# Reordering the pieces of a Fourier convolution stage, loading its first rows a stage ahead, and a third buffer and a new load order in the stage that prepares its spectra

## The reference, cut to what matters

```python
v, x1, x2 = jnp.split(hy, HYENA_ORDER + 1, axis=-1)
filt = hyena_filters(S, ...)                       # (h @ w3) * decay, [L, 2, 2, 1024]
z = v.astype(f32)
for n, gate in enumerate((x1, x2)):
    k = bidir_kernel(filt[:, n, 0], filt[:, n, 1])
    z = gate.astype(f32) * fftconv(z, k, filt_bias[l, n])
```

## Time and profile before

| | |
|---|---|
| three runs | 4445.9, 4446.94, 4450.4 us; median 4446.94 |
| the profiled execution | 4448.89 us, its span 4447.2 us |
| TensorE busy / VectorE busy / ScalarE busy | 3902.3 / 2917.4 / 1788.6 us |
| combining stage | about 1422 to 1607 us of the span |
| Hyena's inputs | up to 2511 us |
| Hyena stage | 2511 to 2964 us |

### The profile page before, as it was taken

One profiled execution on the slowest core, in us unless ns is written; L12 is line 12 of the kernel. 1 busy time (PEld: TensorE's weight loads), 2 busy tenths in 40 slices (PEclk: granted clock), 3 DMA queues, 4 the chain that ended last, 5 costly groups with the idle time before them and its releaser, 6 DMA issues. The chain is left out here.

```text
span 4447.2 us, 43285 instructions
## 1 busy us (share of the span) xinstructions
PE 3902.3 (88%) x16738; PEld 2968.5 (67%) x16738; DVE 2917.4 (66%) x2714; ACT 1788.6 (40%) x1639; POOL 324.8 (7%) x306
## 2 busy tenths in 40 slices
PE   8989988699997878869899787959679999999996
PEld 3558875488875666558788433547468888888884
DVE  3643444788886656642144497865588888888886
ACT  2234321577775325510011101100047777777773
POOL 0000000301110100000000000000000110101100
PEclk9989998799998899979999899979869999999998
DMA  2001025899997421132122523234539999999996
GB/s 105 1 19 29 14 82 190 266 398 398 399 399 281 175 79 48 35 104 90 52 87 88 186 90 129 74 114 149 187 137 370 377 371 380 374 376 377 370 383 226
DMA packets 426674, 890.81 MB, mean 200 GB/s; under 512 B 23036, under 2 KB 119636, under 8 KB 425401
## 3 DMA queue, kind: packets, MB, share of 16 engines
q1 hardware_dynamic: 384088, 758.80, 47.5%
q0 software_dynamic: 28304, 100.73, 6.6%
q10 hardware_dynamic: 14160, 29.63, 1.7%
HBM read 788.67 MB, written 100.43 MB: 200 GB/s over the span
## 5 line engine op out<-in xcount | busy, mean ns | idle before, releaser
L1781 DVE TENSOR_TENSOR moe_w_rest<-moe_w_w,moe_upper 128x2048 fp32r<-128x2048 f32 x384 | 862.6, 2288 | 181.1 <-ACT moe_upper L1709 104.1
L1709 ACT ACTIVATE moe_upper<-moe_w_w 128x2048 fp32r<-128x2048 f32 x192 | 357.2, 1908 | 275.8 <-PE moe_y_ps L1673 106.8
L1781 DVE TENSOR_TENSOR moe_w_rest<-moe_w_w,moe_upper_w 128x2048 fp32r<-128x2048 f32 x192 | 431.1, 2287 | 17.4 <-ACT moe_upper_w L1724 17.1
L1724 ACT ACTIVATE moe_upper_w<-moe_w_w 128x2048 fp32r<-128x2048 f32 x192 | 357.4, 1910 | 138.0 <-PE moe_up_ps L1657 86.3
L1717 ACT ACTIVATE moe_upper<-moe_w_w 128x2048 fp32r<-128x2048 f32 x192 | 357.0, 1917 | 1.7 <-DMA moe_w_w<-in_expert_w_dram 0.9
L1657 PE MATMUL moe_up_ps<-moe_upper,moe_x_upper 128*128 128x512 f32 x768 | 311.5, 406 | 0.0
L1657 PE MATMUL moe_gate_ps<-moe_upper,moe_x_upper 128*128 128x512 f32 x768 | 306.0, 398 | 4.7 <-DVE moe_x_rest L1794 4.7
L1673 PE MATMUL moe_y_ps<-moe_upper_w,moe_hidT_upper 128*128 128x512 f32 x768 | 305.3, 398 | 4.2 <-DVE moe_hidT_rest L1799 3.8
L1657 PE MATMUL moe_gate_ps<-moe_w_rest,moe_x_upper 128*128 128x512 f32 x768 | 305.4, 398 | 0.0
L1657 PE MATMUL moe_gate_ps<-moe_upper,moe_x_rest 128*128 128x512 f32 x768 | 305.3, 398 | 0.0
L1673 PE MATMUL moe_y_ps<-moe_upper_w,moe_hidT_rest 128*128 128x512 f32 x768 | 303.7, 395 | 0.0
(11 more groups left out here) (504 smaller groups left out, 7792.2 us busy)
## 6 DMA issues: line engine op xcount, KB each, us to landing
moe_w_w<-in_expert_w_dram SPq DMA_DIRECT2D x96, 2048.0 KB, 16.5
moe_w_w<-in_w_gate_dram SPq DMA_DIRECT2D x64, 2048.0 KB, 10.6
moe_w_w<-in_w_up_dram SPq DMA_DIRECT2D x64, 2048.0 KB, 9.4
moe_w_w<-in_w_down_dram SPq DMA_DIRECT2D x64, 2048.0 KB, 9.1
tmp_y_rows<-moe_y ACTq DMA_DIRECT2D x32, 512.0 KB, 7.0
hyin_w<-in_w_in_dram SPq DMA_DIRECT2D x24, 512.0 KB, 3.8
tmp_h<-out_xn POOLq DMA_DIRECT2D x16, 512.0 KB, 3.2
tmp_spectra<-held_K ACTq DMA_DIRECT2D x8, 1024.0 KB, 5.0
```

The source lines that it names most:

```text
L1709: act.activation(half(upper1(c), h), half(weights.w1[c % 2], h), ACT.Copy).then_inc(m.w1_rounded, 1)
L1724: act.activation(half(upper2(c), h), half(weights.w2[c % 2], h), ACT.Copy).then_inc(m.w2_rounded, 1)
L1781: dve.tensor_tensor(half(rest, h), half(whole, h), half(upper, h).bitcast(F32), ALU.subtract).then_inc(done, 1)
```

## The change

1. Hyena stage, TensorE's list is now `U00 U01 U10 F1 K10 K11 I0 U11 U20 I1 U21 F3 U30 K30 I2 K31 U31 I3`. VectorE's loop is as before, except that the weights of both made passes are summed at the start, in place, and not one before and one behind F1.
2. The first three chunks of input rows belong to the tables and are loaded behind them, in the stage before (`load_rows`). The four first decay tiles are no longer loaded there; SP loads them first in the Hyena stage.
3. Combining stage: three K buffers instead of two. A copy waits for the store of unit u-3.
4. Combining stage: SP's order is weights, decay, x of tile 0, transform table, gains, x of tile 1; VectorE adds tile 0, multiplies the first filters by the decay, then adds tile 1 and only there waits for the gains. The weights are summed in place, with four instructions instead of two.

```diff
             @block.sync
             def _(sp):
                 held.load_weights(sp)
+                held.load_decay(sp, 0)
...
                     sp.dma_start(x[b][:, :], x1[bass.ts(t, P), :]).then_inc(x_loaded[b], 16)
                     if t == 0:
+                        held.load_table(sp)
                         for j, gain in enumerate((gain1, gain2)):
                             sp.dma_start(g[j][:, :], row(gain).partition_broadcast(P)).then_inc(g_loaded, 16)
-                        held.load_decay(sp, 0)
-                    elif t == 1:
-                        held.load_table(sp)
...
-                held.sum_weights(dve)
-                dve.wait_ge(g_loaded, 32)
+                held.sum_weights(c)
...
                 add(0)
+                held.decay_filters(c, 0)
                 for t in range(NT):
                     b = t % 2
                     if t + 1 < NT:
                         add(t + 1)
+                    if t == 0:
+                        dve.wait_ge(g_loaded, 32)
                     norm(x[b], 0, t, n1[b], n1_ready)
-                    if t % HF == 0:
+                    if t and t % HF == 0:
                         held.decay_filters(c, t // HF)
...
                 repeat(sp, N_ALL // 2, load)
                 next_tables.load(sp)
+                for b in NB:
+
+                    sp.wait_ge(stored[b], 16 * (HY_W // P // 2))
+                next_tables.load_rows(sp, v_x1)
...
+        for o in range(HY_ORDER):
+            w = m.w3[0:FILT_HID, o]
+            add_to(c, w[:, SUM, :], w[:, DIFF, :])
+            dve.scalar_tensor_tensor(w[:, DIFF, :], w[:, DIFF, :], -2.0, w[:, SUM, :], ALU.mult, ALU.add).then_inc(m.w3_summed, 1)
...
     def copy(m, act, u):
-        fh = u % HF
-        if u >= HF:
-
-            act.wait_ge(m.stored[fh], 16 * (u // HF))
+        b = u % m.N_K
+        if u >= m.N_K:
+
+            act.wait_ge(m.stored[b], 16 * (u // m.N_K))
...
-        for t in range(N_DECAY):
-            m.load_decay(sp, 0, t)
         sp.dma_start(m.inv[:, :, :, :, :], m.inverse).then_inc(m.inv_loaded, 16)
+
+    def load_rows(m, sp, v_x1):
+        for b in range(N_CHUNKS):
+            sp.dma_start(m.u[b][:, :, :], residues(v_x1, RESIDUE[b], 0)).then_inc(m.u_loaded[b], 16)
...
-    program = [("U", 0, 0), ("U", 0, 1)]
-    for n in range(1, NP):
-        if n in MADE:
-            program += [("F", n, 0), ("K", n, 0), ("U", n, 0), ("I", n - 1, 0), ("K", n, 1), ("U", n, 1)]
-        else:
-            program += [("U", n, 0), ("I", n - 1, 0), ("U", n, 1)]
-    program += [("I", NP - 1, 0)]
+    program = [("U", 0, 0), ("U", 0, 1), ("U", 1, 0), ("F", 1, 0), ("K", 1, 0), ("K", 1, 1), ("I", 0, 0), ("U", 1, 1), ("U", 2, 0),
+               ("I", 1, 0), ("U", 2, 1), ("F", 3, 0), ("U", 3, 0), ("K", 3, 0), ("I", 2, 0), ("K", 3, 1), ("U", 3, 1), ("I", 3, 0)]
...
                     for i in SLOTS:
                         v = RADIX * (HF * n + fh) + i
+                        if v < N_CHUNKS:
+                            continue
...
+                for t in range(N_DECAY):
+                    load_decay(0, t)
                 for what, n, fh in program:
...
-                    if nth + 1 < len(MADE):
-                        sum_w3(nth + 1)
...
-                sum_w3(0)
+                for nth in range(len(MADE)):
+                    sum_w3(nth)
                 butterflies(0, 0, None)
```

More of the change, by code:

```diff
@@ L2079, in _ @@
                     act.wait_ge(stored[b], 16 * (NT // 2))
-                    act.wait_ge(held.stored[b], 16 * (NT // 2))
+                held.wait_stored(act)
             @block.tensor
@@ L2990, in __init__ @@
         super().__init__(nc, "held")
-        self.hidden, self.w3, self.bias_src, self.decay_src, self.forward, self.spectra = hidden, w3, bias, decay, forward, spectra
+        self.hidden, self.w3_src, self.bias_src, self.decay_src, self.forward, self.spectra = hidden, w3, bias, decay, forward, spectra
     def __enter__(m):
@@ L3002, in __enter__ @@
         m.filt = m.sb("filt", [P, 2, HJ, RADIX, HS])
-        m.K = [m.sb(f"K{fh}", [P, RADIX, 2, HS]) for fh in range(HF)]
+        m.K = [m.sb(f"K{b}", [P, RADIX, 2, HS]) for b in range(m.N_K)]
         m.filt_ps = [m.ps(f"filt_ps{b}", [P, 2, HS]) for b in range(2)]
@@ L3018, in __enter__ @@
         m.ready = m.sem("ready")
-        m.stored = [m.sem(f"stored{fh}") for fh in range(HF)]
+        m.stored = [m.sem(f"stored{b}") for b in range(m.N_K)]
         return m
@@ L3058, in make_filters @@
             for d in (SUM, DIFF):
-                last = m.nc.tensor.matmul(m.filt_ps[f % 2][:, d, :], m.hid_T[:, bass.ts(t, P)], m.w3_sum[:, o, d, bass.ts(s, m.HS)], start=True, stop=True)
+                last = m.nc.tensor.matmul(m.filt_ps[f % 2][:, d, :], m.hid_T[:, bass.ts(t, P)], m.w3[:, o, d, bass.ts(s, m.HS)], start=True, stop=True)
             last.then_inc(m.filt_made, 1)
@@ L3113, in store, with wait_stored, residues @@
         o, s = m.BLOCKS[u // HF]
+        b = u % m.N_K
         act.wait_ge(m.ready, u + 1)
-        act.dma_start(m.spectra[o, u % HF][:, :, :, bass.ts(s, m.HS)], m.K[u % HF][:, :, :, :]).then_inc(m.stored[u % HF], 16)
-N_DECAY = 4
+        act.dma_start(m.spectra[o, u % HF][:, :, :, bass.ts(s, m.HS)], m.K[b][:, :, :, :]).then_inc(m.stored[b], 16)
+    def wait_stored(m, act):
+        for b in range(m.N_K):
+            act.wait_ge(m.stored[b], 16 * len(range(b, HF * len(m.BLOCKS), m.N_K)))
+N_DECAY, N_CHUNKS = 4, 3
 PASSES = [(o, h) for o in range(HY_ORDER) for h in range(HY_W // HC)]
 MADE = [n for n, (o, h) in enumerate(PASSES) if h not in HELD_HALVES]
+def residues(x, r, h, part=0):
+    rows = x.rearrange("(j p r) c -> r p j c", p=P, r=RADIX)[r]
+    return rows[:, :, bass.ds(part * HY_W + h * HC, HC)]
 class HyenaTables(Store):
@@ L3144, in open @@
         m.bias_loaded = [m.sem(f"bias_loaded{nth}") for nth in range(len(MADE))]
[L3145 removed]
+        m.u_loaded = [m.sem(f"u_loaded{b}") for b in range(N_CHUNKS)]
         m.k_loaded = [m.sem(f"k_loaded{fh}") for fh in range(HF)]
@@ L3201, in hyena_phase @@
     with Store(nc, "hyena") as m:
-        w3_sum = m.sb("w3_sum", [P, 2, HC])
+        decay_sb = [m.sb(f"decay{b}", [P, HC]) for b in range(N_DECAY)]
         filt = m.sb("filt", [P, 2, HJ, RADIX, HC])
-        u = [m.sb(f"u{b}", [P, HJ, HC]) for b in range(N_CHUNKS)]
         U = [m.sb(f"U{b}", [P, RADIX, 2, HC]) for b in range(N_U)]
@@ L3210, in hyena_phase @@
         inv_ps = [m.ps(f"inv_ps{b}", [P, HC]) for b in range(2)]
-        u_loaded = [m.sem(f"u_loaded{b}") for b in range(N_CHUNKS)]
+        decay_loaded = [m.sem(f"decay_loaded{b}") for b in range(N_DECAY)]
         gate_loaded = [m.sem(f"gate_loaded{b}") for b in range(2)]
@@ L3226, in hyena_phase @@
         N_F = 2 * NT
-        def residues(x, r, h, part=0):
-            rows = x.rearrange("(j p r) c -> r p j c", p=P, r=RADIX)[r]
-            return rows[:, :, bass.ds(part * HY_W + h * HC, HC)]
         def channels(x, h, cb):
```

72 lines of the change are left out of this document (35 added, 37 removed).

## The result

| | before | changed kernel |
|---|---|---|
| median of the runs | 4446.42 us (4 runs) | 4419.77 us (4 runs, 4417.84 to 4421.18) |
| ratio | | 0.9938, 95% interval 0.9921 to 0.9955 |
| profiled execution, its span | 4448.89, 4447.2 us | 4417.84, 4416.2 us |
| combining stage | 184.70 us | 169.69 us |
| last input of the stage ahead of Hyena made, to Hyena's first issue | 10.48 us | 8.37 us |

What follows compares the result with a forecast made beforehand. VectorE's chain, waiting for TensorE's pieces, bounds the Hyena stage; in the combining stage TensorE waits for ScalarE's copies. Hyena 16.8 plus combining 13.5 make 30.3 us off 4446.9: about 4416.6 us, range 4409 to 4430.

Steps and rivals of the forecast that it cites:

- Rows ahead: Hyena stage start: with input rows loaded a stage earlier, U00 starts about 0.2 us behind the barrier, 3.8 us gained.
- The shift of the barrier: End of the stage before Hyena: changed load traffic shifts it by 0, between 1.3 us later and 2.6 us earlier.
- Rival 3: The stage before Hyena ends later, its last store counted only after all issued loads: 4418 to 4420 us, chance 0.1.
- Sums of w3: Hyena stage, VectorE: four summing instructions at the start lie under the wait for U00, 1.2 us gained.
- F1: Hyena stage, filters: a TensorE that paused less may serve the first ones faster; taken as 0, 2 us kept for range.
- K11 and U11 ahead of need: Hyena stage: VectorE's waits of 6.50 and 6.28 us go, about 1.0 us comes back at I0's results: 11.8 us gained.
- K31 and U31: Hyena stage, last pass: both still come behind I2, so the waits of the last pass stay.
- Rival 1: Hyena waits come back in I0, which has no margin: 6.5 us lag, sum 24 us, 4423 us, chance 0.12.
- Rival 5: Hyena stage: TensorE at half clock in K10, K11 and I0, slower, up to 69 us, 4485 us; chance 0.02.
- Third K buffer: Combining stage: ScalarE's copies 3 and 5 start 6.51 and 2.21 us sooner, unit 7 gains 1.10 us: 9.8 us.
- Start of the combining stage: Combining stage: first filters end 6.8 us sooner, 3.1 us back behind ScalarE's norms: net 3.7 us, between -1 and 6.5.
- Rival 2: Combining stage: new load order gains nothing, gains and tile 1 landing 5 us late: 4.7 us less, 4421 us, chance 0.13.

## Why the prediction was right, and where its terms were wrong

The time forecast was 4416.6 us, 3 below what was measured, with the sign and nearly the size. That the sum came so close is partly luck, as the terms show, by the prediction's own steps:

- *Rows ahead, 3.8 us.* 4.1 in the profile and 4.5 by the experiment. Right.
- *The shift of the barrier, 0.* The stage's end came 2.1 us sooner, which was inside the range of 1.3 later to 2.6 sooner. The last store issued landed in 6.3 us and not in 8.4, which is that difference. Putting the rows back into their own stage makes it 0.7 shorter still. So the added rows cost 0.7 us and leave some 2.8 (2.1 + 0.7) for the decay taken away; that this is its doing is inferred, no run has it alone. The section of the Trainium skill that the prediction weighed (DMA: Bandwidth & Descriptors, Queues, rings and completion order), read widely, wanted the end later; this case's profile has it sooner, with the rows issued later than any other load and landing 28.2 us after issue. Rival 3 did not come.
- *Sums of w3, 1.2 us,* and *F1, 0.* The sums left the path; but from VectorE's first product with the decay to the end of the filters F1 took 19.2 us where it took 17.9. The step's reason, that a TensorE that pauses less would serve F1 faster, did not hold: TensorE's pause ahead of the 28 records went from 21.15 to 7.42 us and nothing was gained, and with the old list, where the pause is 21.14 us again, F1 takes 19.1. So the 1.3 us against the profile before come neither from the order nor from the length of this pause; what they come from is not shown. A pause of 7.42 us was long enough for the lower clock, and F1 began with 0.52 to 0.63; with the pause filled its 28 records took 13.86 us and F1 16.7.
- *K11 and U11 ahead of need, 12.8 less 1.0.* The two waits went, all of the 12.8 us. "About 1 us more" for I0's results was 2.8, since the price of K was taken from K10 alone, at full clock, while in the new kernel K10 starts at 0.66 and K10 with K11 cost 1.7 more. The trace of before held the warning, in a row of TensorE's timeline that I had not weighed, K30 behind the same pause:

```profile
2786.11 22.53 PE L3328 MATMUL hyena_fwd_ps<-hyena_filt,hytab_tr 128*128 128x512 f32 x48 [2.26 <-issue]
```

22.53 us for the same 48 records that took 20.84 in K10. The runs show the term by itself: 0.59 us of wait with the pause filled, 2.29 without.
- *"I1 starts when VectorE is done, as before, with TensorE cold as before."* Cold, but longer cold. Moving U20 forward made TensorE's pause ahead of I1 29.34 us instead of 22.34. The clock over the first 6 us of I1 was 0.50, and 0.66 before, and the wait for its first result 4.72 us instead of 3.32. That is 1.4 us which the step did not have.
- *K31 and U31: "the waits of the last pass stay".* U31's did (9.48 us both times). K31's grew from 3.71 to 5.11, because I2's last 96 records took 22.67 us where they had taken 21.32. All six profiles of the new order without extra matmuls have 22.67, so it is a cost of the order, 1.4 us. The step overlooked that taking away the pause of 2.26 us in front of K30 puts one in front of I2, where TensorE had gone on without a pause. Before and after:

```profile
2822.22 7.07 PE L3370 MATMUL hyena_inv_ps<-hytab_inv,hyena_U 128*128 128x256 f32 x32
2831.68 21.32 PE L3370 MATMUL hyena_inv_ps<-hytab_inv,hyena_U 128*128 128x256 f32 x96 [2.40 <-DVE hyena_z L3452]
```

```profile
2789.57 8.86 PE L3383 MATMUL hyena_inv_ps<-hytab_inv,hyena_U 128*128 128x256 f32 x32 [2.64 <-DVE hyena_U L3521]
2800.42 22.67 PE L3383 MATMUL hyena_inv_ps<-hytab_inv,hyena_U 128*128 128x256 f32 x96 [1.99 <-DVE hyena_z L3463]
```

The clock over 2800 to 2805 us was 0.66, and 1.00 in the same place before. But the new pause alone does not settle it: with extra matmuls in earlier pauses it is still there, and four kernels of five were back at 21.3. The rest of the cause is open.

Hyena: 12.0 us, plus 2.1 at the barrier, where 16.8 were forecast. The terms come to 11.2 (4.1 + 1.2 - 1.3 + 12.8 - 2.8 - 1.4 - 1.4); the other 0.8 lies behind the wait for U31 (75.5 us to the stage's end before, 74.7 after). The prediction had called a wait over 1 us ahead of I0's first result a sign against it, and it came. Rival 1 (the waits come back in I0, for want of margin) was right in that the margin is nothing, but its size was 6.5 us and the measured one is 2.3, three quarters of it from the clock. Rival 5, half clock in K10, K11 and I0, was right in kind and small: 1.7 us, half of what it counts for one group of eight records, where it needed nine groups.

- *Third K buffer, 9.8 us.* 12.1 by the experiment, 13.9 by the profiles of before and after (125.27 and 111.41 us from the second block of filters to the stage's end). The gaps gave 9.6 and 10.0, as forecast; what was missing is that the records behind a long gap run slowly, 3.1 us in the experiment and 4.3 in the kernel before (9.82 and 8.86 us instead of twice 7.17).
- *Start of the combining stage, 3.7 us.* About 0 by the experiment, 1.1 by the profiles of before and after. The first transform was sooner by 5.5 and not 6.8 us, because x of tile 0 landed later than worked out: VectorE's first addition started 17.7 us into the stage where the forecast had 16.6. And the 3.1 us given back at the third transform was 2.65 of wait and 1.5 of clock. Against the old start beside it nothing is left. Rival 2 was near in its size (4.7 us less, 3.7 measured); its reason (late gains) was wrong, since nothing waited for them. The reason was the give-back that the forecast had named and priced too low.

Combining: 15.0 us in the two profiles (13.9 + 1.1), some 12 by the experiments, where 13.5 were forecast. The stage gains of the two profiles, 12.0, 2.1 and 15.0, make 29.1; the medians leave 26.7. Equal code differs by up to 4.6 us in the combining stage from profile to profile and the kernel before has one profile, so the difference probably lies there, which is not shown. The sum came out because errors of both signs cancelled. Apart from the 2.1 us at the barrier and the 1.1 us by which x was late, most of them come from one missing item, the clock that TensorE has after a pause. It can make a new pause dearer than its length and a removed one worth more than its length.

## What to carry to other kernels

When a change moves work on an engine whose clock falls in pauses, list the pauses before and after, and give each two prices: its length alone, and its length with the records behind it at the rate of a cold start seen in the same trace. Pauses of 2.3 to 2.7 us went both ways here, the one of 7.13 us cost 3.1 us more than its length. When a wait is taken away by doing work early, ask what the early work now leaves empty; here it was the stretch ahead of I1. A new order can gain nothing until the engine next in line (ScalarE with its norms) is reordered too: the two together gave some 3 to 4 us, the first alone none.

## What was unexpected in the hardware

A pause of 2.26 us was enough for TensorE to come back below full clock. In all ten profiles of the new order that have the pause between F1 and K10, the 96 records behind it took 43.13 or 43.14 us, and with 1.7 us of unneeded work in the pause 41.44. With the old order the 48 records behind such a pause took 22.4 to 22.5 us in three cases of four (K10 and K30, in the kernel before and in the experiment) and 20.84 us in the one that the prediction was built on. What sets that one apart is not shown.

Unneeded matmuls whose results nobody reads made a kernel faster by some 7 us of 440, in that they only filled pauses; a filling that stopped 0.5 to 1.6 us ahead of the useful work was close enough.
